# A two-layer decoder trunk: the feed-forward in two halves of the tokens, its up-projection by one level of Strassen's algorithm

## What is computed

```python
D_MODEL = 1024; D_FF = 4096; SEQ = 1024; N_META = 16; DEC_BATCH, DEC_SEQ = 8, 4; DEPTH = 2
def sqrelu_mlp(h, w_up, w_down):
    return jnp.square(jax.nn.relu(h @ w_up)) @ w_down
# in each layer i: x += mixer(rms_norm(x, norm_mix[i]));  x += sqrelu_mlp(rms_norm(x, norm_mlp[i]), mlp_w_up[i], mlp_w_down[i])
```

## Time and profile before

| | us |
|---|---|
| median of 3 runs | 2403.19 (2401.75 to 2403.48) |
| the profiled execution, its own time | 2403.05 |
| its span | 2400.9 |
| PE busy | 2376.8 |
| DVE, ACT, POOL busy | 1005.1, 571.1, 112.2 |

### The profile page before, as it was taken

How to read it: one execution, slowest core, us unless ns; L and a number is a source line. 1 busy time by engine, 2 the same in 40 slices (tenths; PEclk the granted TensorE clock), 3 DMA queues, 4 the chain that set the end, 5 groups by cost and what they waited for, 6 DMA issues and landing times.

```text
span 2400.9 us, 35144 instructions
## 1 busy us (share of the span) xinstructions
PE 2376.8 (99%) x15129; PEld 2313.5 (96%) x15129; DVE 1005.1 (42%) x1408; ACT 571.1 (24%) x1016; POOL 112.2 (5%) x131
## 2 busy tenths in 40 slices
PE   8999999999999999999999999999999999999998
PEld 8997899999999999999999998889999999999998
DVE  6449724433433433335623325545343333333433
ACT  6549722111111111103310116422111111110111
POOL 1005400000000000000000004100000000000000
PEclk9999999999999999999999999999999999999999
DMA  8622031111101111111321136431111111111102
GB/s 227 85 47 73 11 100 52 37 53 35 52 35 52 46 41 52 35 52 35 113 53 36 40 103 178 141 117 38 51 53 35 52 37 50 52 35 52 35 35 72
DMA packets 133011, 150.21 MB, mean 63 GB/s; under 512 B 33421, under 2 KB 107177, under 8 KB 132764
## 3 DMA queue, kind: packets, MB, share of 16 engines
q1 hardware_dynamic: 129980, 136.11, 19.3%
q0 software_dynamic: 2720, 12.56, 1.7%
q10 hardware_dynamic: 224, 0.30, 0.0%
HBM read 126.50 MB, written 24.47 MB: 63 GB/s over the span
## 4 chain that ended last, share of the span: by engine, by line
PE 96%; DVE 1%; ACT 1%; issue 0%; DMA 0%; DVEq 0%
PE ps L310 42%; PE ps L316 21%; PE ps L296 8%; PE ps L299 7%; PE ps L297 7%; PE ps L544 1%; PE ps L1026 1%; PE ps L1002 1%; PE ps L983 1%; ACT prob L1094 1%; PE ps L2065 1%; PE ps L1403 1%; PE ps L1404 1%; PE ps L1405 1%; PE ps L2046 1%; PE ps L2050 1%
## 5 line engine op out<-in xcount | busy, mean ns | idle before, releaser
L1530 DVE TENSOR_TENSOR x<-x,ps 128x1074 f32<-128x1074 f32 (+1 forms) x128 | 161.8, 1264 | 460.8 <-PE ps L316 460.8
L264 ACT ACTIVATE w_hi<-raw 128x1024 fp32r<-128x1024 f32 x180 | 187.3, 1050 | 650.8 <-PE ps L316 484.9
L310 PE MATMUL ps<-act_hi,w_lo 128*128 128x358 f32 (+1 forms) x1536 | 334.0, 325 | 0.0
L310 PE MATMUL ps<-act_hi,w_hi 128*128 128x358 f32 (+1 forms) x1536 | 333.7, 325 | 0.0
L310 PE MATMUL ps<-h_hi,w_hi 128*128 128x358 f32 (+1 forms) x1536 | 333.4, 325 | 0.0
L310 PE MATMUL ps<-h_hi,w_lo 128*128 128x358 f32 (+1 forms) x1536 | 333.1, 325 | 0.0
L316 PE MATMUL ps<-act_lo,w_hi 128*128 128x358 f32 (+1 forms) x1536 | 272.1, 324 | 0.0
L1512 DVE SCALAR_TENSOR_TENSOR relu<-ps,rstd 128x1074 f32<-128x1074 f32 (+1 forms) x64 | 81.1, 1267 | 447.5 <-PE ps L316 447.5
L310 PEld LDWEIGHTS ps<-act_hi,w_hi 128*128 128x128 f32 x1536 | 263.9, 189 | 0.0
L310 PEld LDWEIGHTS ps<-act_hi,w_lo 128*128 128x128 f32 x1536 | 263.9, 189 | 0.0
L316 PE MATMUL ps<-h_lo,w_hi 128*128 128x358 f32 (+1 forms) x1536 | 263.6, 326 | 0.0
(11 more groups left out here) (324 smaller groups left out, 2363.2 us busy)
## 6 DMA issues: line engine op xcount, KB each, us to landing
raw<-in_mlp_w_up SPq DMA_DIRECT2D x32, 1024.0 KB, 5.7
raw<-in_mlp_w_down SPq DMA_DIRECT2D x32, 1024.0 KB, 5.0
raw<-in_mlstm_w_in SPq DMA_DIRECT2D x12, 1024.0 KB, 5.4
x<-scratch_x SPq DMA_DIRECT2D x8, 537.0 KB, 6.1
scratch_x<-x POOLq DMA_DIRECT2D x1, 4296.0 KB, 14.1
x<-scratch_x SPq DMA_DIRECT2D x8, 528.0 KB, 4.9
x_tok<-in_x_prompt SPq DMA_DIRECT2D x8, 512.0 KB, 7.8
raw<-in_attn_w_qkv SPq DMA_DIRECT2D x16, 256.0 KB, 7.3
```

The lines of the kernel that those rows point to most:

```text
L264: nc.scalar.activation(unit_view(w_hi, slot, down), raw_unit(j, rslot, down), ACT.Copy).then_inc(w_hi_ready, 1)
L310: nc.tensor.matmul(ps[:, bank + g, 0:width], w_block(w, slot, k, kc, cols), hi[:, k, g * width:g * width + width], start=start and i == 0, ...
L1530: nc.vector.tensor_tensor(view(x[:, o, :]), view(x[:, o, :]), ps[:, out_banks(n):out_banks(n) + 3, 0:w], ALU.add).then_inc(out_free, 1)
```

## The change

The feed-forward now goes over the tokens in two halves (536 columns in layer 0, 528 in layer 1), and each half over the 8 slices: 16 runs per layer instead of 8 slices, every weight loaded and split once per half. In a run the up-projection works on two pairs; a pair is 256 hidden features. A pair's weights are a 2 x 2 grid of blocks (two halves of the depth, two tiles of features), and the tokens of the half are two quarters of q = 268 (264) columns, so the pair's product is a 2 x 2 block product. It is done by Strassen's algorithm in Winograd's form, with seven block products (`product_pe`) in place of eight; each has 4 depth tiles and three matmuls of q columns per tile, all into one bank. Four of the seven weight operands of a pair have to be computed as sums or differences of blocks, which POOL does from `raw` (`sum_pool`, 512 elements per partition each); the operands on the token side are computed once per half, by DVE (`b_dve`, 11 steps of 4q elements) and ACT (`b_hi_act`). The seven results are combined by DVE in 13 steps (`up_take_dve`), eleven of them of q elements and two of 2q. Steps 7, 9 and 12 are the relu times rstd of what the step before made, as step 5 is; step 8 needs product 6, step 11 product 7; steps 10 and 13 are the squares of 2q elements. An `act_lo` step of 2q elements follows each square. The down-projection has 8 outputs of 24 matmuls of q columns. The feed-forward's input is no longer split as `h_hi` and `h_lo`; `b_scale_act` multiplies x with the gain, and the operands of the products are made from that. The waits for POOL's last stores stand behind its sums.

```diff
+RUNS = 2 * SLICES
+RUN_SPLITS = 18
...
+        def sum_pool(pool, pair, k, first):
+            if k in (1, 3):
+                pool.wait_ge(w_summed, first + (1 if k == 1 else 2))
+            a11, a12, a21, a22 = (raw_part(pair, *kn) for kn in ((0, 0), (1, 0), (0, 1), (1, 1)))
+            s1, s2 = (w_part(w_sum, j) for j in (1, 2))
+            dst = w_part(w_sum, (1, 2, 3, 5)[k])
+            in0, in1, op = ((a21, a22, ALU.add), (s1, a11, ALU.subtract), (a11, a21, ALU.subtract),
+                            (a12, s2, ALU.subtract))[k]
+            nc.gpsimd.tensor_tensor(dst, in0, in1, op).then_inc(w_summed, 1)
...
+        def mlp_pool(pool, layer, half, i, more=True):
...
+            for k in range(4):
+                pool.wait_ge(up_ready, ups((2, 3, 4, 6)[k]))
+                sum_pool(pool, 1, k, sums(4))
...
+        def up_take_dve(dve, layer, half, i, pair, step, ups, taken):
+            q, first, second = up_views(layer, pair)
+            x0, z0, y0, y1 = (up_bank(layer, pair, w)[:, 0:q] for w in range(4))
...
+            if step == 1:
+                dve.wait_ge(up_ready, ups(7 * pair + 3))
+                dve.wait_ge(up_copied, mlp_copies(layer, half, i)(pair + 1))
+                ins = nc.vector.tensor_tensor(second, first, y0, ALU.add)
+            elif step == 2:
+                dve.wait_ge(up_ready, ups(7 * pair + 4))
+                dve.wait_ge(up_taken, taken(done + 1))
+                ins = nc.vector.tensor_tensor(m2[:, 0:q], second, y1, ALU.add)
+            elif step == 3:
+                dve.wait_ge(up_taken, taken(done + 2))
+                ins = nc.vector.tensor_tensor(m2[:, q:2 * q], m2[:, 0:q], z0, ALU.add)
+            elif step == 4:
+                ins = nc.vector.tensor_tensor(m1[:, q:2 * q], second, z0, ALU.add)
+            elif step == 5:
+                dve.wait_ge(up_taken, taken(done + 3))
+                ins = relu_of(m2[:, q:2 * q], m2[:, q:2 * q], late)
+            elif step == 6:
+                dve.wait_ge(up_ready, ups(7 * pair + 5))
+                ins = nc.vector.tensor_tensor(m1[:, 0:q], first, x0, ALU.add)
...
...
+        def mlp_up_dve(dve, layer, half, i):
+            up_lo_dve(dve, 1, 0, w(7 + 1))
+            take(0, 1, 2, 3, 4, 5, 6, 7)
+            dve.wait_ge(w_summed, sums(6))
+            up_lo_dve(dve, 1, 1, w(7 + 2))
+            up_lo_dve(dve, 1, 3, w(7 + 3))
+            up_lo_dve(dve, 1, 4, w(7 + 4))
+            take(0, 8, 9, 10)
+            act_lo_dve(dve, layer, 0, 0, taken, acts)
+            dve.wait_ge(w_summed, sums(8))
+            up_lo_dve(dve, 1, 2, w(7 + 5))
+            up_lo_dve(dve, 1, 5, w(7 + 6))
+            take(0, 11, 12, 13)
+            act_lo_dve(dve, layer, 0, 1, taken, acts)
+            up_lo_dve(dve, 1, 6, w(7 + 7))
+            take(1, 1)
+            mlp_down_lo(dve, 0, w(15))
+            take(1, 2, 3, 4, 5, 6, 7)
+            mlp_down_lo(dve, 1, w(16))
+            take(1, 8, 9, 10)
+            act_lo_dve(dve, layer, 1, 0, taken, acts)
+            take(1, 11, 12, 13)
+            act_lo_dve(dve, layer, 1, 1, taken, acts)
+            mlp_down_lo(dve, 2, w(17))
+            mlp_down_lo(dve, 3, w(18))
...
+        def product_pe(pe, layer, half, pair, item, bank, waits):
...
+            pe.wait_ge(w_lo_ready, waits(7 * pair + ITEM_AT[item] + 1))
+            pe.wait_ge(b_by_act, b_count(layer, half, 7) + item + 1)
+            for k in range(4):
+                for n, w in enumerate((w_hi, w_lo)):
+                    nc.tensor.matmul(o, w_part(w, item)[:, k, :], hi[:, k, :], start=k == 0 and n == 0,
+                                     stop=False)
+            pe.wait_ge(b_by_dve, by_dve + (2, 3, 7, 8, 9, 10, 11)[item])
+            for k in range(4):
+                last = nc.tensor.matmul(o, w_part(w_hi, item)[:, k, :], lo[:, k, :], start=False, stop=k == 3)
+            last.then_inc(up_ready, 1)
...
+                for item, bank in ((0, 0), (1, 1), (2, 2), (3, 3), (4, 0), (5, 1), (6, 3)):
...
+                    elif item == 4:
+                        pe.wait_ge(up_copied, mlp_copies(layer, half, i)(pair + 1))
+                    elif item == 5:
+                        pe.wait_ge(up_taken, taken(13 * pair + 4))
+                    product_pe(pe, layer, half, pair, item, bank, w)
+                    if first and pair == 0 and item == 2:
+                        for g in range(3):
+                            norm_pe(pe, 2 * layer + 1, g)
...
+                for ks in ((0, 1), (2,), (3,)) if o == 0 else (range(4),):
+                    if o == 0:
+                        pe.wait_ge(act_split, acts(ks[-1] + 1))
+                    for k in ks:
+                        passes(k, w_hi, act_hi, k == 0, False)
+                        passes(k, w_lo, act_hi, False, False)
+                    for k in ks:
+                        last = passes(k, w_hi, act_lo, False, k == 3)
...
+        def b_first_dve(dve, m, n0):
+            dve.wait_ge(out_ready, n0 + KC)
+            for j in range(1, 4):
+                b_dve(dve, m // 2, 0, j)
+            norm_acc_dve(dve, m, KC - 1)
+            for j in range(4, B_STEPS):
+                b_dve(dve, m // 2, 0, j)
```

More of the change, by code:

```diff
@@ L304, in w_block @@
             return w[:, slot, :].rearrange("p (k n) -> p k n", k=kc)[:, k, cols]
[L306 to L318, removed]
         def pe_unit(pe, u, n, hi, lo, sides=None, first_norm=None, side_at=(2, 4, 6), w=TG):
-            pe.wait_ge(w_lo_ready, u + 1)
+            pe.wait_ge(w_lo_ready, splits_through(u))
             if n >= 2:
@@ L1437, in project_dve @@
                 if c >= 2:
                     norm_acc_dve(dve, m, c - 1)
+                if c == KC - 2:
+                    b_dve(dve, m // 2, 0, 0)
                 dve.wait_ge(x_back[c], 32)
                 add_x_dve(dve, n0 + c, c, x, m)
-            dve.wait_ge(out_ready, n0 + KC)
[L1442 to L1450, removed]
+            first_up_lo_dve(dve, U_MLP0, KC)
@@ L1451, in mlp_slice_sp @@
+        def mlp_slice_sp(sp, layer, half, i):
+            u0, done = (U_MLP0, U_MLP1)[layer], mlp_splits(layer, half, i)
             up = a["mlp_w_up"][layer].rearrange("(k p) n -> p k n", p=P)
@@ L1478, in mlp_split_lo @@
[L1478 to L1524, removed]
-                else:
[L1526 to L1539, removed]
@@ new lines, in b_first_of, with b_count, b_scale_act @@
+        def b_first_of(layer):
+            return b_first[layer][:, 0:4 * QT[layer]].rearrange("p (k n) -> p k n", k=4)
+        def b_count(layer, half, steps):
+            return steps * (2 * layer + half)
+        def b_scale_act(act, layer, half, f, x):
+            m = 2 * layer + 1
+            nc.scalar.activation(b_gained[layer][:, f, 0:2 * QT[layer]], x[:, f, half_cols(layer, half)], ACT.Copy,
+                                 scale=gains[:, gain_of[m], f:f + 1]).then_inc(b_scaled, 1)
@@ new lines, in up_bank, with up_views, up_copy_act @@
+        def up_bank(layer, pair, which):
+            return ps[:, 4 * pair + (which if layer == 0 else (3, 0, 1, 2)[which]), :]
+        def up_views(layer, pair):
+            q = QT[layer]
+            return q, up_sum[pair][:, 0, 0:q], up_sum[pair][:, 1, 0:q]
+        def up_copy_act(act, layer, pair, ups):
+            q, first, _ = up_views(layer, pair)
+            act.wait_ge(up_ready, ups(7 * pair + 1))
+            nc.scalar.activation(first, up_bank(layer, pair, 0)[:, 0:q], ACT.Copy).then_inc(up_copied, 1)
@@ new lines, in mlp_up_dve, with take @@
+        def mlp_up_dve(dve, layer, half, i):
+            ups, taken, sums, w, acts = (c(layer, half, i) for c in (mlp_ups, mlp_taken, mlp_sums, mlp_splits, mlp_acts))
+            def take(pair, *steps):
+                for step in steps:
+                    up_take_dve(dve, layer, half, i, pair, step, ups, taken)
+            up_lo_dve(dve, 1, 0, w(7 + 1))
[22 more added lines that the diff above has]
+            mlp_down_lo(dve, 3, w(18))
@@ L1585, in build, with mlp_run_pe @@
+        def mlp_run_pe(pe, layer, half, i, first=False):
+            mlp_up_pe(pe, layer, half, i, first)
+            mlp_down_pe(pe, layer, half, i)
         ROWB = 4320
@@ L2574, in _ @@
                     x2_load_f(sp, 7)
-            with sp.Fori(0, SLICES) as i:
-                mlp_slice_sp(sp, 1, U_MLP1, i)
+            for half in range(2):
+                with sp.Fori(0, SLICES) as i:
+                    mlp_slice_sp(sp, 1, half, i)
             y_store(sp)
```

601 lines of the change are left out of this document (480 added, 121 removed).

## The result

The kernel after takes 2527.8 us (median of 4 runs, 2526.2 to 2528.0), the one before 2402.5 (2401.6 to 2403.5): ratio 1.0519, interval 1.0507 to 1.0532, slower by 125.3 us. The profiled execution has a span of 2524.3 us, 123.4 over the 2400.9 of before.

What follows compares the result with a forecast made beforehand. Before, PE's column count bounds the feed-forwards; after, DVE's chain was to make PE wait. From 2403 us, +87 for steady runs and +31 for starts and seams gave 2521, stated as 2522, range 2425 to 2610.

Steps and rivals of the forecast that it cites:

- DVE-bound with PE waiting at three named places: PE waits at product 10, product 13 and before the first down output's last 6 matmuls; 122 to 130 ns; chance 0.63.
- Matmul price: Feed-forward matmuls on PE cost column time plus 15.1 ns: 126.8 ns in layer 0, 125.1 in layer 1.
- the 127 that the prediction names as a sign: Matmul spacing in the down phase was to be 127 ns; 114 would speak for cheaper matmuls.
- The first rival: Shorter feed-forward matmuls run at the plain fp32 price, 93 us off, 2429 us; chance 0.10 together with the page's-rule variant, 2433.
- DVE's chain: DVE's list from up_take step 2, after the fourth product, to the last act_lo takes 21.4 us per layer 0 run.
- Stalls: PE loses 1.0 us at product 10, 1.8 at product 13, 1.5 before the first down output's last 6 matmuls.
- PE's busy time: Over the whole kernel PE's share falls to some 92%, with PE busy near 2325 us.
- "DVE works its list in order and never idles": From up_take step 2 to the last act_lo, DVE runs back to back, 21.4 us, and so sets the run.
- Edges: Feed-forward starts +14.5 and +11 us, turns to the second half and norm tail +2 each: together +31, bounds +10 to +50.
- A turn between halves: Turning to the second half puts 11 b_dve steps into one down phase: +2 us each.
- Rival 2: DVE's chain is hidden by overlapping fixed costs and PE alone sets the run: 2382 us, chance 0.13.
- Rival 3: POOL sums drift into DVE's SBUF stretches, 3 more blocks a run, 2618 us, chance 0.10; sign: repeatedly stretched DVE splits.

Runs made afterwards that it cites:

- Runs without gaps: Kernel after with down outputs 0 and 1 side by side, all four float32 squares on ACT, DVE reordered by due times: 2401.3 us.
- run 24: Not a run label: the words say that in the down phase of a run without gaps, 24 matmuls start in 2.96 us.
- The late second split: Kernel after with DVE's second down-projection weight split moved behind the last act_lo: 2521.8 us.
- the thin sums: Kernel after with POOL's weight sums on 8 of every 128 columns, waits and order kept: 2481.3 us.

## Why the prediction was right

Predicted 2522, measured 2527.8. DVE-bound with PE waiting at three named places was the likeliest case, and it is what happened. That the two numbers are so close is partly luck: the steady runs cost 9 us less than forecast and the edges 14 more.

- **Matmul price.** Predicted 126.8 and 125.1 ns. Runs without gaps give 45.24 / 360 = 125.7 and 44.73 / 360 = 124.3 ns. That is columns plus a constant, with 14 ns for 15. Inside the down phase of such a run 24 matmuls start in 2.96 us, 123.3 ns each for the 127 that the prediction names as a sign. The first rival (113.7) falls. What the Trainium skill (TensorE: Matmul & The Clock Gate, section Back-to-back issue gap) gives for an isolated matmul, columns / 2.4 + 2.5 ns or 114.2 ns, is not met either. The prediction took that figure for one of a stream; the section has lower ones for streams with weight loads (81 ns at 128 columns, 131 at 512), and the 164.3 ns at 358 columns disagree with those too.
- **DVE's chain.** 21.4 us predicted, 21.7 measured. Two things in it were larger than priced: act_lo starts 0.12 us behind its square (673.42 for a square shown to 673.29), not 0.03, four times; and POOL's block is 1.09, not 1.0.
- **Stalls.** 1.0, 1.8 and 1.5 us predicted, 4.3 in all; 0.71, 1.66 and 1.41 in the brackets, 4.37 in all by the run without gaps (49.61 - 45.24). Run 49.9 predicted, 49.61 measured; layer 1 49.4 and 49.19. In sum +87 predicted, +78.2 measured. PE's busy time was to fall to near 2325 us and is 2343.8: a run with gaps shows 45.69 us busy and one without 44.97, some 23 us over 32 runs, because a gap shows only from the modelled end of the matmul before it.
- **"DVE works its list in order and never idles"** was true as a count and too simple as a cause. The late second split shows that from step 4 on the path crosses to PE and back (product 13), so of 1.14 us of DVE work that was taken out only 0.19 came back. That does not move the forecast, but it would have misled anyone who cut DVE work there.
- **Edges.** The term that was mis-sized: +31 predicted, 45.2 measured. A turn between halves was put at 2 us and takes 49.29 + 55.47 for 2 x 49.61, 5.5 us; DVE's steps there take up to 2.36 us for 1.27 beside POOL's sums, which the prediction counted in steady runs and not here, and the thin sums took those 5.4 us away again. That is +7 over both layers. The rest lies at the starts. From the first matmul to the end of the wait before the last block of down output 0 a layer's first run takes 47.4 us in layer 0 (392.66 to 440.10) and 45.1 in layer 1 (1698.24 to 1743.31), where steady runs take 28.0 and 27.8. Less 1.8 for the norm's matmuls, that is +17.6 and +15.5 for the +14.5 and +11 predicted, 7.6 us more. In layer 0 DVE reaches step 2 at 418.37, 25.7 us behind the projection for 22.5 worked out. The waits of PE there are 4.64, 2.73, 3.54 and 1.71 us, and the granted clock behind the first is 0.55 to 0.8:

```profile
396.00:402.00 6.00, 3.54 (x16) 0.55 0.52 175
402.00:408.00 6.00, 3.27 (x15) 0.78 0.00 0
408.00:414.00 6.00, 4.34 (x18) 0.81 0.00 0
414.00:420.00 6.00, 2.40 (x13) 0.76 0.00 0
```

  How much of the 7.6 us is this clock and how much the order was not separated.
- **Rival 2** (a hidden chain) was not to be had by overlap, but can be made by hand: without the gaps the time is 2401, not 2382, because the edges cost more than the 31 us that rival counted. Rival 3 (drifting POOL sums) did not occur: DVE's chain has one block a run, as laid out. The sums for the next run's pair 0 do stretch three splits of the down part (692.91, 699.66 and 704.78 in layer 0 take 1.17, 1.67 and 1.24 us for 0.69), so "more than once a run" was a poor sign; DVE has time there, and the steady run is no longer for it.

## What to carry to other kernels

A Strassen level trades multiplications for additions on slower engines; before counting columns saved, lay the helper engines' list between the first product that they need and the last result that the tensor engine needs, at its own durations, and compare that with the tensor engine's time there. An engine that shows no idle time need not be the path: look at what the next dependent step would have waited for, and move one operation to find out. When the steady state is mended, the edges decide: here 63 us saved in steady runs against about as much spent at the edges, most of it at two starts and two turns.

## What had not been expected of the hardware

Two PE gaps of 0.96 and 1.40 us, with only six matmuls between them, were followed by the lower granted clock (0.50, 1.2 GHz) for 3 to 4 us in most runs, while single gaps of 1.41 or 1.66 us, some 7 us from start to start, left it at 1.00. The 2.4 us of waiting then cost 1.5 us more. It is not certain to happen: in four of layer 1's runs gaps of 0.99 and 1.38 us left the clock at 1.00. A longer pause did it alone: behind the gap of 5.68 us at the turn in layer 0 the clock was

```profile
816.00:822.00 6.00, 0.48 (x4) 0.82 0.52 176
822.00:828.00 6.00, 5.84 (x31) 0.61 0.01 3
828.00:834.00 6.00, 6.00 (x51) 1.00 0.01 2
```

Single gaps of some 2 us were followed by it in some runs and not in others. With two more operations in the up part, product 10 waits that long; one such gap, and the clock behind it (last row: length, PE busy, granted clock, DMA share, GB/s):

```profile
682.49 0.39 PE L1961 MATMUL ps<-b_hi_low,w_hi 128*128 128x268 f32 x1 [1.99 <-DVE w_lo L1542]
...
684.00:686.00 2.00, 2.00 (x11) 0.50 0.00 0
```

Where DVE sets the end anyway, a slower PE ahead of a wait costs little. In that kernel about half of the windows of one run have a clock of 0.97 and the others of 1.00, and runs of layer 0 take 50.86 us with either: where the clock fell, the wait before product 13 shrank from 1.66 to some 0.25 us.
